# Row numbers, masks, sample weights and query copies of the attention input move from VectorE to GpSimd and ScalarE

## The reference

```
def indexer_topk(qi, wi, ki, q_pos, n_keys, topk):
    s = jnp.einsum('bqhd,bsd->bqhs', qi, ki, preferred_element_type=jnp.float32)
    score = jnp.einsum('bqhs,bqh->bqs', jax.nn.relu(s), wi.astype(jnp.float32)) * IDX_SCALE
    causal = jnp.arange(n_keys)[None, :] <= q_pos[:, None]
    score = jnp.where(causal[None], score, -jnp.inf)
    _, idx = lax.top_k(score, topk)
    valid = idx <= q_pos[None, :, None]
    return idx, valid
...
    in_past = idx < past
    pidx = jnp.minimum(idx, past - 1)
    phys = jnp.take_along_axis(page_table, (pidx // PAGE_SIZE).reshape(db, -1), axis=1).reshape(idx.shape)
    off = pidx % PAGE_SIZE
    def pick(pool, new):
        old = pool[layer, phys, off].astype(new.dtype)
        return jnp.where(in_past[..., None, None], old, gather(new, nidx))
    return sparse_attend(q, pick(pool_k, k_new), pick(pool_v, v_new), valid)
```

## Time and profile before

| what | value |
|---|---|
| median of 3 runs | 596.62 us (596.24 to 596.82) |
| the profiled execution's span, first to last instruction | 594.4 us |
| TensorE busy | 579.6 us (98%) |
| VectorE, ScalarE, GpSimd busy | 458.9, 368.9, 218.1 us |
| granted TensorE clock | 0.997 of full |

### The profile page before, as it was taken

How to read it: one execution, slowest core, us unless ns; L and a number is a source line. 1 busy time by engine, 2 the same in 40 slices (tenths; PEclk the granted TensorE clock), 3 DMA queues, 4 the chain that set the end, 5 groups by cost and what they waited for, 6 DMA issues and landing times.

```text
span 594.4 us, 12739 instructions
## 1 busy us (share of the span) xinstructions
PE 579.6 (98%) x5015; PEld 501.6 (84%) x5015; DVE 458.9 (77%) x927; ACT 368.9 (62%) x625; POOL 218.1 (37%) x213
## 2 busy tenths in 40 slices
PE   7999998999999999999999999999999999999995
PEld 6888787988888888888888888888888888888885
DVE  4799899556887887788668898799887778785542
ACT  6974566576675656565555788846765656564322
POOL 3242328723264545451011112233554545432220
PEclk9999999999999999999999999999999999999998
DMA  9949668319776766688997962065766767779602
GB/s 264 276 120 267 197 181 267 109 53 293 242 207 188 205 188 201 186 235 229 264 267 212 250 180 72 1 178 156 202 202 191 202 189 205 226 214 243 181 8 74
DMA packets 205421, 113.29 MB, mean 191 GB/s; under 512 B 5561, under 2 KB 202217, under 8 KB 205337
## 3 DMA queue, kind: packets, MB, share of 16 engines
q1 hardware_dynamic: 203169, 106.33, 63.1%
q0 software_dynamic: 1680, 5.79, 3.0%
q10 hardware_dynamic: 512, 0.35, 0.2%
HBM read 108.83 MB, written 3.86 MB: 190 GB/s over the span
## 4 chain that ended last, share of the span: by engine, by line
PE 76%; DVE 16%; ACT 4%; issue 2%; DMA 1%; POOL 1%; ACTq 0%; DVEq 0%; SPq 0%
PE acc L1543 23%; PE acc L1540 23%; PE acc L1537 23%; DVE w_lo L986 5%; ACT w_hi L592 1%; DVE area L1116 1%; PE misc L1898 1%; PE acc L1727 1%; DVE scratch L1066 1%; PE acc L1729 1%; PE acc L1728 1%; DMA area<-in_x_prompt 1%; DVE area L1067 1%; PE misc L1665 1%; DVE aL L995 1%
## 5 line engine op out<-in xcount | busy, mean ns | idle before, releaser
L1537 PE MATMUL acc<-aH,w_hi 128*128 128x264 f16 (+1 forms) x886 | 244.5, 276 | 1.3 <-DVE work L1315 0.7
L1540 PE MATMUL acc<-aL,w_hi 128*128 128x264 f16 (+1 forms) x886 | 244.5, 276 | 0.0
L1543 PE MATMUL acc<-aH,w_lo 128*128 128x264 f16 (+1 forms) x886 | 244.5, 276 | 0.0
L986 DVE SCALAR_TENSOR_TENSOR w_lo<-stage,w_hi 128x1024 f16<-128x1024 f32 (+1 forms) x155 | 204.7, 1326 | 28.9 <-ACT w_hi L592 28.8
L592 ACT ACTIVATE w_hi<-stage 128x1024 f16<-128x1024 f32 (+1 forms) x155 | 171.2, 1110 | 33.1 <-PE acc L1543 25.2
L1537 PE MATMUL acc<-zH,w_hi 128*128 128x264 f16 x384 | 106.0, 276 | 0.0
L1540 PE MATMUL acc<-zL,w_hi 128*128 128x264 f16 x384 | 106.0, 276 | 0.0
L1543 PE MATMUL acc<-zH,w_lo 128*128 128x264 f16 x384 | 106.0, 276 | 0.0
L1540 PEld LDWEIGHTS acc<-aL,w_hi 128*128 128x128 f16 (+1 forms) x886 | 88.1, 99 | 13.5
L1537 PEld LDWEIGHTS acc<-aH,w_hi 128*128 128x128 f16 (+1 forms) x886 | 86.8, 98 | 15.0 <-issue 2.4
L1543 PEld LDWEIGHTS acc<-aH,w_lo 128*128 128x128 f16 (+1 forms) x886 | 88.1, 99 | 12.6
(11 more groups left out here) (422 smaller groups left out, 943.7 us busy)
## 6 DMA issues: line engine op xcount, KB each, us to landing
stage<-in_w_ffn_up SPq DMA_DIRECT2D x88, 512.0 KB, 4.6
stage<-in_w_ffn_down SPq DMA_DIRECT2D x32, 704.0 KB, 5.9
stage<-in_w_attn_in SPq DMA_DIRECT2D x22, 512.0 KB, 6.0
stage<-in_w_rec_in SPq DMA_DIRECT2D x16, 512.0 KB, 5.2
stage<-in_w_attn_out SPq DMA_DIRECT2D x8, 512.0 KB, 5.0
stage<-in_w_rec_out SPq DMA_DIRECT2D x8, 512.0 KB, 3.9
area<-in_w_attn_in SPq DMA_DIRECT2D x4, 512.0 KB, 4.9
area<-in_x_prompt SPq DMA_DIRECT2D x2, 512.0 KB, 4.8
```

Source lines behind the costliest of these rows:

```text
L986: v.scalar_tensor_tensor(low, stage[:, place_in_line(u) % 4, 0:n, 0:cols], WSCALE, high, ALU.mult, ALU.subtract).then_inc(lo_done, 1)
L1537: t_.matmul(out, high[:, c, :], xH[:, x0 + c, :], start=first and c == 0, stop=False)
L1540: t_.matmul(out, high[:, c, :], xL[:, x0 + c, :], start=False, stop=False)
L1543: ins = t_.matmul(out, low[:, c, :], xH[:, x0 + c, :], start=False, stop=last and c == n - 1)
```

## The change

Five things move. (1) Row numbers go to GpSimd (`row_numbers`, step 12); the part that depends on the page table alone is done once at the start. (2) The masks and the new token's flag go to GpSimd (`biases`, step 15). (3) `wblk`, the samples' head weights, goes to GpSimd (step 5). (4) Four small copies of the index queries into `qz` go to ScalarE (step 6). (5) The two identity sums `lane` and `own` go to the front of VectorE's program. Besides, `rope(12)` runs one search round earlier, the number picking moves to VectorE's step 14, ahead of its search rounds, and `turn_picked` stands one matmul later in unit 14. A semaphore `searched` tells GpSimd when the sample search (1) and the last search of all (2) are done.

```
-                    dve.wait_ge(qz_zero, 1)
-                    for half in range(2):
-                        ...
-                            ins = v.tensor_copy(places[:, b:b + 3:2, :], qiT[ID * b:ID * b + ID, :, TP:T])
-                    ins.then_inc(ki_twice, 1)
...
+                if u == 6:      # ScalarE
+                    act.wait_ge(qz_zero, 1)
+                    act.wait_ge(roped, 3)
+                        ...
+                            ins = nc.scalar.copy(places[:, b:b + 3:2, :], qiT[ID * b:ID * b + ID, :, TP:T])
+                    ins.then_inc(ki_twice, 1)
                     act.wait_ge(idx_mm, 2)
...
+            dve.wait_ge(const_in, 16)
+            v.tensor_reduce(lane[:], ident.rearrange("p (s r) -> p r s", s=NS), AX.X, ALU.add)
+            v.tensor_reduce(own[:], ident.rearrange("p (s r) -> p s r", s=NS), AX.X, ALU.add)
             dve.wait_ge(ones_set, 1)
             dve.wait_ge(x_in[1], 16)
...
+                if u == 14:
+                    dve.wait_ge(phys_turned, 1)
+                    small(v.tensor_tensor(picked..., C[:, 0:P]..., lane[:]..., ALU.mult))
+                    small(v.tensor_reduce(gbias[:], picked..., AX.X, ALU.add))
+                    v.tensor_copy(gix[:], gbias[:, 0:4]).then_inc(gix_done, 1)
                 if 13 <= u < 16:
-                    take_second(2)
+                    take_second(2, last=u == 15)
...
-                    take_merged(6, 2)
-                if u == 12:
-                    ...
+                    take_merged(6, 1)
+                    rope(12)
+                    take_merged(7, 1, found=True)
...
-                        between = lambda i: turn_picked() if i == 6 else None
+                        between = lambda i: turn_picked() if i == 8 else None
...
+            def row_numbers():
+                pool.wait_ge(searched, 1)
+                small(g.tensor_copy(idxf[:], i8[0:NS, :]))
+                small(g.tensor_scalar(idxt[:], idxf[:], float(PAGE), pt8f[:, 3:4], ALU.is_ge, ALU.mult))
+                small(g.tensor_scalar(pf[:, 0:64], idxf[:], float(PAST - 1), pt8f[:, 0:1], ALU.min, ALU.add))
+                g.tensor_tensor(pf[:, 0:64], pf[:, 0:64], idxt[:], ALU.add).then_inc(phys_done, 1)
+                g.tensor_scalar(pf[:, 64:128], idxf[:], float(PAST), OUT_OF_REACH, ALU.is_equal, ALU.mult).then_inc(phys_done, 1)
+
+            def biases():
+                pool.wait_ge(searched, 2)
+                g.tensor_scalar(abias[64:P, 0:P], mscore[64:P, 0:P], TAKEN, OUT_OF_REACH, ALU.is_gt, ALU.mult).then_inc(bias_done, 1)
+                pool.wait_ge(bias_done, 1)
+                g.tensor_scalar(abias[:, P:384], score[:, P:384], TAKEN, OUT_OF_REACH, ALU.is_gt, ALU.mult).then_inc(bias_done, 1)
+                pool.wait_ge(bias_done, 2)
+                small(g.tensor_scalar(selnew[:], mscore[0:NS, PAST:PAST + 1], TAKEN, OUT_OF_REACH, ALU.is_gt, ALU.mult))
+                g.tensor_scalar(seld[:], ident[0:NS, 0:NS], selnew[:, 0:1], None, ALU.mult).then_inc(phys_done, 1)
...
+                if u == 12:
+                    row_numbers()
+                if u == 15:
+                    biases()
                 if u == RAW_V[-1]:
                     pool.wait_ge(gix_done, 1)
                     for j in range(4):
                         gather(a["cache_k"], kgat, kg_in, j)
```

## The result

| | before | changed |
|---|---|---|
| median of 5 runs on one chip | 596.62 us (596.07 to 596.82) | 600.19 us (600.0 to 600.68) |
| ratio to before | | 1.0063, 95% interval 1.0053 to 1.0074 |
| span of the profiled execution | 594.4 us | 598.5 us |
| its time | not recorded; the median is 2.2 us above the span | 600.35 us |

The changed kernel is 3.6 us slower, twice the 1.8 forecast and 0.2 us outside the range. Of the 4.1 us between the two spans 0.55 us is no part of that: TensorE's first transposes of x began at 9.84 us in the profiled execution and at 9.29 in the one of before, and the third group of experiments shows that this is chance. The times agree: in every recorded execution of before and of the changed kernel about 1.8 us lie outside the span, so the profiled execution of before was some 0.4 us under its median, and that of the changed kernel 0.16 above.

The account below looks back on a forecast made before the run. VectorE's queue was taken to set the clock from the first sample dot. The dot starts at the later of 72.0 (VectorE) and 76.4 (gather), against 74.60: +1.8 us, 596.2 plus 2.2 outside the span, 598.4 us; range 595.4 to 600.0.

Parts of the forecast that it names:

- whatever moves the start of `sample_dots(0)` moves TensorE's program by as much: VectorE's queue sets the clock from the first dot, 74.60 us, to key 2's transpose, 90.86; nothing later returns a shift.
- the cost of the masks: Four GpSimd mask steps between the last search and the first gather: 1.6 us, bounds 0.5 and 2.5.
- the up to 0.8 us by which a `lo` stretches GpSimd's work: First key gather beside `lo(19)`: 1.79 us instead of 1.01, so up to 0.8 on top of its landing.
- Search end at 69.2: VectorE's last search round ends at 69.2 us, and GpSimd's `biases` ahead of the gathers waits for it.
- the 0.9 us ahead that was taken: VectorE's assumed lead at the seventh search round, begun at 57.05 before, letting `rope(12)` run at 57.6 us.
- Gather to first dot, 5.3: First key gather issued at 71.1 us, landing 4.4 to 4.8 later plus up to 0.8 stretch; first dot at 76.4.
- TensorE's waits of some 4 us in three: Expected profile sign: waits in the transposes of keys 0, 1 and 2 grow from 1.5 us in two.
- At nothing: Moves costed at zero: identity sums ahead of x, query copies on ScalarE, `wblk` on GpSimd; masks' later readers unaffected.
- The 0.5 us won at 65.26: TensorE's 0.48 us wait behind ScalarE's value-unit copy goes, but becomes a longer wait for the keys' rotations.
- VectorE could start the dots at 72.0: VectorE finishes `lo(19)` at 72.0 us, ready for the first dot 2.6 us early.
- rival "faster": Last search ends much earlier, gather back by 72 us, TensorE loses its waits: 2.0 us gained, 594.6; chance 0.13.
- rival "the slack covers it": Cheap masks and a 4.4 us landing put the gather at 74.4, dots start as now: 596.6 us; chance 0.13.

Follow-up runs that it names:

- the third group of experiments: The runs e4 and e9, which put some of the change's other moves (not the masks alone) back on VectorE: 599.9 and 595.34 us.
- e4: The changed kernel with the two identity sums back in VectorE's step 5: 599.9 us, ratio 1.0059 to before.
- e12: The changed kernel with its two masks made as products by constants 1 and 1 (outputs wrong): 599.42 us, ratio 1.0045.
- e5: The kernel before with only the masks and flag moved to GpSimd's step 15, ahead of the gathers: 602.93 us, ratio 1.0115.
- e3: The changed kernel with all masks back on VectorE in step 16, only `gix` ahead of the gathers: 594.77 us, ratio 0.9976.
- e8: e3 with the third sample's dot products one step later, behind `rope(19)` and `lo(23)`: 595.0 us, ratio 0.9976.
- e9: e3 with identity sums, query copies and samples' weights also back on VectorE: 595.34 us, ratio 0.9978.
- e7: The kernel before with only the rotation of unit 12 one sample-search round earlier: 596.02 us, ratio 0.9991.
- e2: e1 with one added wait, for the last search's end, ahead of the key gathers, no mask between: 597.3 us, ratio 1.0015.
- e11: e3 with both the later third-sample dots of e8 and the earlier masks of e10: 594.51 us, ratio 0.9968.
- e10: e3 with VectorE's masks before `lo(19)`, in its wait for `hi(19)`: 594.32 us, ratio 0.9965.
- e13: The changed kernel with its two masks made as products by two identity columns (outputs wrong): 600.59 us, ratio 1.0063.
- e1: The changed kernel with three mask steps right behind the row numbers and the 128x256 mask behind the key gathers: 594.81 us, ratio 0.9975.

## Why the prediction was wrong in size and right in kind

The whole argument can be tested by one subtraction, span less start of the first dot: 519.8 us before, 519.7 changed, 519.7 in e4, 519.7 in e12, 519.8 in e5, 519.8 in e3 and e8, 519.9 in e9. The step "whatever moves the start of `sample_dots(0)` moves TensorE's program by as much" holds in these, over dots from 73 to 81 us. Six profiled executions lie above: 520.2 in e7, 520.4 in e2 and e11, 520.8 in e10 and e13, 521.0 in e1. Part of that is a wait of another kind, for the last gather of values, in TensorE's first products with values. The same three starts in the kernel before and in e2:

```profile
102.75 0.28 PE L1665 MATMUL misc<-pb,area 128*128 128x8 f32 x2
103.00 0.28 PE L1665 MATMUL misc<-pb,area 128*128 128x8 f32 x2
103.36 0.28 PE L1665 MATMUL misc<-pb,area 128*128 128x8 f32 x2
```
```profile
102.79 0.28 PE L1658 MATMUL misc<-pb,area 128*128 128x8 f32 x2
103.34 0.39 PE L1658 MATMUL misc<-pb,area 128*128 128x8 f32 x2
103.80 0.28 PE L1658 MATMUL misc<-pb,area 128*128 128x8 f32 x2
```

From the first of these starts to the third it is 0.61 us before (0.62 changed, 0.61 in e3, e4, e5, e8, e11 and e12) and 1.01 in e2. The chain of waits of e2 names the reason:

```profile
95.24 8.05 DMA area<-in_cache_v,gix
```

The same stretch takes 1.05 us in e7, 1.14 in e1, 0.95 in e13 and 0.88 in e10. That is 0.3 to 0.5 us lost behind the keys, which no step of the prediction has; whether it belongs to these kernels or only to these executions, no run shows. What is left above 519.8 is nothing in e7, 0.2 in e2, the second wait in e13, and some 0.7 in the three kernels whose first dot comes before 73 us (e1, e10, e11): there VectorE no longer sets the whole of it.

**The step that failed** is the cost of the masks: "I take 0.35 + 0.62 for the two masks, 0.2 each for the flag and the diagonal, some 0.08 between: 1.6 us", with 2.5 us as the bound from above. They took 3.15 us, outside the bounds:

| | forecast | measured | what the runs showed |
|---|---|---|---|
| 64x128 mask | 0.35 | 0.70 | 0.30 to 0.45 as a product |
| 128x256 mask | 0.62 | 1.11 | 0.41 to 0.56 as a product |
| flag, 8x1 | 0.2 | 0.73 | 0.23 clear of a `lo` |
| diagonal, 8x8 | 0.2 | 0.32 | 1.24 under a `lo` |
| between them | 0.24 | 0.29 | |

The rows taken as nearest were products by factors from memory, and e12 and e13 show that a mask costs up to twice as much as those. And the up to 0.8 us by which a `lo` stretches GpSimd's work was looked for at the gather alone, where it fell on the flag, 0.5 us of it; no term of the masks had it. The masks are 1.55 of the 1.8 us missed, the search's end 0.26.

The rest, laid beside the changed trace less its 0.55 us of chance:
- *Search end at 69.2*: 70.01, so 69.46: 0.26 us late. `rope(12)` ran at 58.67 and not 57.6, because VectorE was not the 0.9 us ahead that was taken: its seventh search round began at 57.30, which is 0.3 ahead of the 57.05 of before when the chance is taken out; but `hi(17)` was made at 63.0, within 0.5 of the 62.0 forecast when the chance is taken out, and so the search end moved little.
- *Gather to first dot, 5.3*: 5.36. The number is right by luck. It was made of 4.8 to the landing and 0.5 for a gather stretched by a `lo`; the gather stood clear of the `lo` (1.10 us), and the landing took 5.22 by the chain of waits. With no stretch either, it took 4.34 in e2 and 5.17 in e4, so the bounds of 4.4 to 4.8 were too narrow; what sets it, no run shows.
- *TensorE's waits of some 4 us in three*: 5.5 in three, more by what the masks took.
- *At nothing*: the sums (e4) and all three small moves (e9). Right, as far as these runs can tell. The 0.5 us won at 65.26 turned into a longer wait, as said.
- *VectorE could start the dots at 72.0*: it ended `lo(19)` at 72.7, 72.15 without the chance. Right. e3 and e1 show what that readiness would have been worth with the gathers in time: not the 2.0 us of the rival "faster" but 1.5.

The sum with these readings in it: 69.46 for the search's end, 3.4 for masks and gaps, 5.36 for the gather, gives 78.2, less 74.60: 3.6 us. Measured by the medians: 3.6. So the mechanism was right, and its largest term was mis-sized.

The rival "the slack covers it" said that 7.2 us of delay are more than 6. By the runs: e2 delays the gather by 6 us against before and the dot comes at 74.37, as before, yet its ratio is 1.0015, which is 0.9 us slower. In its profiled execution the keys are transposed at the same times as before (86.56 and 90.88 against 86.54 and 90.86), and the 0.4 us between the two spans is the wait for the values shown above. The other 0.5 us lies in executions that were not profiled: this one is the fastest of eleven, 0.7 under their median. What held those up stays open. So 6 us was about all the slack there was.

The stretch of GpSimd's work beside a `lo` reaches further than the prediction used it: not only rotations and gathers but each mask step that begins under a `lo` grew by 0.5 to 0.9 us. This agrees with the lock of the Trainium skill's "SBUF — State Buffer", section "SBUF: two separate sides". That section also says that of two such instructions the one that starts first blocks the other fully. The trace does not show this for `lo`: in the changed kernel it began 0.6 us into the 128x256 mask, 0.03 us after its `hi` was made, and took its usual 1.23 us. The measurement decides: here a mask did not hold up a `lo`, and a `lo` held up a mask.

## What to carry to other kernels

An engine that issues transfers is a queue: a wait put ahead of a transfer costs what the transfer's user waits, even when the work behind the wait is short. Before moving work there, write down when each transfer goes out, when its data are used, and the slack between; here some 6 us of slack met 9.5 us of delay. The same work beside the gathers (e1) was free, and returned the gain that the move had meant to bring. And price an instruction by a row of the same operation, not only of the same size; and where it may begin under a VectorE step with two inputs, at its stretched length.

## What was not expected of the hardware

- GpSimd's tensor-scalar at 128x256: 0.41 us for two products by constants, 0.56 by factors from memory, 1.11 for a comparison and a product. At 8x64 a comparison and a product took 0.53 in the rows of the changed kernel.
- TensorE's start-up matmuls took 421 ns each until about 6.7 us and 275 from there on in the execution of before; in that of the changed kernel they took 421 ns beyond 9 us, with the same instructions ahead on TensorE. That is where the chance of 0.55 us above comes from. The granted clock reads 1.00 in both stretches, so that this is a step from 1.2 to 2.4 GHz is not shown by it; for it speaks that 421 to 275 is the ratio by which f16 matmuls are shown in e4 at a granted clock of 0.50 and of 1.00 (430 and 280 ns).
- After one long wait the granted clock can fall to its lower level, 1.2 GHz, and cost nothing. In e4 (stretch, TensorE's busy us, granted clock, DMA share, GB/s), against 1.00 in the changed kernel after the same wait:

```profile
82.00:86.00 4.00, 0.86 (x8) 0.87 0.55 146
86.00:90.00 4.00, 4.00 (x19) 0.50 0.52 134
```

TensorE had stood 3.14 us for the rotated key at 85.87 and went on at half its rate, busy all the time; the next wait, of 1.18 us, was gone instead. Span less first dot is 519.7 in both. In e5 the clock is 0.50 from 88 to 94 us, after a wait of 5.07 us, and span less first dot is 519.8.
